# Order in which the second token group's operands take their buffers, in the SwiGLU stage of a two-layer encoder

## The reference, cut to what matters

```python
hid = jax.nn.silu(jnp.einsum('btd,df->btf', x, wg)) * jnp.einsum('btd,df->btf', x, wu)
return layer_norm(ALPHA * x + jnp.einsum('btf,fd->btd', hid, wd), ln2_g, ln2_b)
```

## Time and profile before

| | |
|---|---|
| median of 3 runs | 3147.59 us (3146.98 to 3153.67) |
| the profiled execution | 3151.21 us, its span 3149.4 us |
| PE busy (matmul) | 2922.8 us, 93% |
| DVE busy | 2149.4 us, 68% |
| POOL busy | 1725.8 us, 55% |
| ACT busy | 1249.3 us, 40% |
| mean granted TensorE clock | 0.961 |

### The profile page before, as it was taken

The page is one execution under the profiler, slowest core; times in us unless marked ns, Lnnn a source line. Parts: engine busy times, 40 slices in busy tenths (PEclk is TensorE's granted clock), DMA queues, the critical chain, the costliest instruction groups (busy, mean ns, idle before and its releaser), DMA issues. The chain is left out here.

```text
span 3149.4 us, 58397 instructions
## 1 busy us (share of the span) xinstructions
PE 2922.8 (93%) x20464; PEld 2660.4 (84%) x20464; DVE 2149.4 (68%) x3877; ACT 1249.3 (40%) x2422; POOL 1725.8 (55%) x1358
## 2 busy tenths in 40 slices
PE   7979998998999999999889699989989999999996
PEld 6956666887999999999879566668779999899996
DVE  6757776666666677777755577776486666877777
ACT  3324434435333344444333334444353333444442
POOL 2323332434766668788632233334266666788886
PEclk9989997999999999999989899989999999999998
DMA  4321114543222213323332211156432222222222
GB/s 170 126 82 42 51 39 152 158 128 129 88 80 84 88 62 101 100 98 101 116 122 94 78 48 41 33 166 179 132 116 81 80 80 80 74 101 97 101 89 88
DMA packets 175821, 304.91 MB, mean 97 GB/s; under 512 B 56080, under 2 KB 97296, under 8 KB 175344
## 3 DMA queue, kind: packets, MB, share of 16 engines
q1 hardware_dynamic: 165088, 271.70, 27.0%
q0 software_dynamic: 10576, 31.14, 2.5%
HBM read 248.34 MB, written 50.38 MB: 95 GB/s over the span
## 5 line engine op out<-in xcount | busy, mean ns | idle before, releaser
L2766 PE MATMUL PS<-xoh,woph 128*128 128x320 f32 (+1 forms) x2464 | 737.2, 299 | 20.9 <-issue 12.0
L2767 PE MATMUL PS<-xol,woph 128*128 128x320 f32 (+1 forms) x2464 | 735.0, 298 | 0.0
L2768 PE MATMUL PS<-xoh,wopl 128*128 128x320 f32 (+1 forms) x2464 | 733.9, 298 | 0.0
L1490 POOL TENSOR_TENSOR wopl<-T,woph 128x512 fp32r<-128x512 f32 x348 | 516.5, 1502 | 153.9 <-ACT woph L1955 153.9
L2766 PEld LDWEIGHTS PS<-xoh,woph 128*128 128x128 f32 x2464 | 467.7, 190 | 24.7 <-issue 18.0
L2767 PEld LDWEIGHTS PS<-xol,woph 128*128 128x128 f32 x2464 | 467.7, 190 | 0.1
L2768 PEld LDWEIGHTS PS<-xoh,wopl 128*128 128x128 f32 x2464 | 467.4, 190 | 0.0
L2766 PE MATMUL PS<-hidh,wdh 128*128 128x320 f32 (+1 forms) x1408 | 419.9, 298 | 11.4 <-DVE hidl L2616 7.8
L1437 POOL TENSOR_TENSOR Pl<-Pf,Ph 128x256 fp32r<-128x256 f32 (+5 forms) x174 | 219.0, 1265 | 384.5 <-DVE Ph L2349 384.5
L1955 ACT ACTIVATE woph<-T 128x512 fp32r<-128x512 f32 x348 | 217.3, 632 | 522.1 <-DVE T L2611 306.6
L2768 PE MATMUL PS<-hidh,wdl 128*128 128x320 f32 (+1 forms) x1408 | 419.1, 298 | 0.0
(11 more groups left out here) (476 smaller groups left out, 6642.7 us busy)
## 6 DMA issues: line engine op xcount, KB each, us to landing
ru<-in_W_FF SPq DMA_DIRECT2D x88, 512.0 KB, 4.0
rd<-in_W_FF SPq DMA_DIRECT2D x176, 256.0 KB, 2.6
rg<-in_W_FF SPq DMA_DIRECT2D x82, 512.0 KB, 4.1
sqt_scratch<-sqTs POOLq DMA_DIRECT2D x18, 512.0 KB, 4.2
hc<-out_H SPq DMA_DIRECT2D x18, 512.0 KB, 3.8
out_H<-yo POOLq DMA_DIRECT2D x18, 512.0 KB, 3.0
dkraw<-in_CKVT SPq DMA_DIRECT2D x16, 520.0 KB, 4.7
QS<-sqt_scratch SPq DMA_DIRECT2D x16, 512.0 KB, 3.5
```

The costliest lines, as they stand in the source:

```text
L1490: pool.tensor_tensor(wopl[k][:, :, :], w_whole(w, k, first), f(woph[k][:, :, :]), ALU.subtract)\
L2766: pe.matmul(out, wh, mh, start=start, stop=False)
L2767: pe.matmul(out, wh, ml, start=False, stop=False)
L2768: return pe.matmul(out, wl, mh, start=False, stop=stop)
```

## The change

The buffers of group 1 are taken in another order, and casts, sums and rests are placed to fit: A11 and A12 take the first two buffers (free with products 7 and 8), then S1, S2, S3, S4, and A22 takes the last. ACT casts A11 and A12 at steps 8 and 9 of turn 10, the sums at steps 10 to 13, and A22 at step 0 of turn 11. POOL takes the rests of A11 and A12 at steps 9 and 10 (before: 12 and 13), and that of A22 at step 0 of turn 11 (before: 1), one weight rest earlier. DVE builds the sums at steps 9 to 12, behind the step's weight sums (before: steps 7 to 10, ahead of them), takes the rests of S1, S2, S3 at steps 11, 12, 13 of turn 10 (before: S2 and S1 at 11 and 12, S3 at step 0 of turn 11), and that of S4 at step 2 of turn 11 as before. No instruction is added or dropped.

```diff
-X_SLOT = ((0, 1, 2, 3, 4, 5, 6), (4, 5, 1, 0, 2, 6, 3))
-X_BY_ACT = ((0, 1, 5, 3, 2, 6, 4), (3, 2, 4, 6, 0, 1, 5))
+X_SLOT = ((0, 1, 2, 3, 4, 5, 6), (0, 1, 3, 2, 4, 6, 5))
+X_BY_ACT = ((0, 1, 5, 3, 2, 6, 4), (0, 1, 3, 2, 4, 6, 5))
 X_BY_DVE = (("lo0", "lo1", "S1", "S2", "S4", "lo2", "lo3", "S3", "lo4", "lo5", "lo6", "g9", "x9"),
-            ("S1", "S2", "S3", "S4", "lo2", "lo3", "lo4", "lo6"))
+            ("S1", "S2", "S3", "lo3", "S4", "lo2", "lo4", "lo6"))
...
# POOL, turn
-                        if no == PAIRS - 1 and i in (12, 13):
-                            x_op_lo(i - 12)
-                        if no == PAIRS and i == 1:
+                        if no == PAIRS - 1 and i in (9, 10):
+                            x_op_lo(i - 9)
+                        if no == PAIRS and i == 0:
                             x_op_lo(5)
...
# ACT, turn
-                            x_op_hi(1, {8: 3, 9: 2, 10: 4, 11: 6, 12: 1, 13: 5}[i])
-                        if no == PAIRS - 1 and i == 11:
-                            x_op_hi(1, 0)
+                            x_op_hi(1, {8: 0, 9: 1, 10: 3, 11: 2, 12: 4, 13: 6}[i])
+                        if no == PAIRS and i == 0:
+                            x_op_hi(1, 5)
...
# DVE, turn
-                        if no == PAIRS and i in (0, 2):
-                            x_op_lo(1, 4 + i)
+                        if no == PAIRS and i == 2:
+                            x_op_lo(1, 6)
...
-                        if no == PAIRS - 1 and i in (7, 8, 9, 10):
-                            x_sum(1, (3, 2, 4, 6)[i - 7])
...
-                        if no == PAIRS - 1 and i in (11, 12):
-                            x_op_lo(1, i - 9)
+                        if no == PAIRS - 1 and i in (9, 10, 11, 12):
+                            x_sum(1, {9: 3, 10: 2, 11: 4, 12: 6}[i])
+                        if no == PAIRS - 1 and i >= 11:
+                            x_op_lo(1, {11: 3, 12: 2, 13: 4}[i])
```

## The result

The changed kernel took 3158.2 us (median of 20 runs, 3147.6 to 3167.3), the kernel before 3150.9 (20 runs, 3146.6 to 3159.3): a ratio of 1.0018 with a 95% interval of 1.0011 to 1.0026, that is 3.5 to 8.2 us slower. A second timing of both gave 1.0021 (1.0008 to 1.0035). The forecast was +5.9 us; the measured ratio is +5.7, the two medians are 7.3 apart, and so are the two profiled spans.

What follows compares the result with a forecast made beforehand. PE, busy 93% of the span, was taken as the bound, with DVE second and in arrears. PE's three waits go, DVE's arrears replace them: +2.95 us a layer, 3147.6 + 5.9 = 3153.5 us, range 3146 to 3159.

Steps and rivals of the forecast that it cites:

- The three waits of PE: Turn 11's products waiting for POOL's rests of A11, A12 and A22: waits of 3.04, 2.79 and 0.71 us would go.
- DVE's 2.2 us of new idle: Step 8 of turn 10: without the S1 and S2 sums DVE waits 1.36, 0.42 and 0.42 us for PE's products.
- The S1 sum of 3.4 us: Step 9 of turn 10: DVE's sum, 1.17 us of work, takes 3.4 because POOL's A11 rest holds SBUF first.
- rival B: Every moved instruction keeps its own row's duration, so POOL's rests cost DVE no more: 3149.4 to 3150.2 us; chance 0.13.
- PE's new waits: Down products 12, 14, 15, 0 and 2 wait for DVE: 1.1, 1.05, 4.3, 4.6 and 2.7 us, 13.8 a layer.
- the walk: Instruction-by-instruction reckoning of the hand-over, POOL and DVE taking turns at SBUF: down product 4 at 2760.80, old order 2757.85.
- The sum: Down product 4 compared between new and old order, both reckoned alike: +2.95 us a layer, +5.9 for two layers.
- the list of today's waits: PE's waits in the kernel before, from the trace: 8.5 us a layer, 10.4 with slow products and slower starts.
- The clock: Half-clock spells behind PE's new waits, costly over product 5: 0 to +1.6 us a layer, taken as 0.
- Rival C: The clock falls behind the new waits too, in both layers: 3155 to 3157 us; chance 0.18.
- Rival A: DVE keeps up at addition 13 and hid_lo, so the change is faster: 3130 to 3142 us; chance 0.14.
- Rival D: The order doesn't bite: another operand still comes last and PE's waits add up as before, 3147.6 us; chance 0.05.

Runs made afterwards that it cites:

- e2: Kernel before with its buffers, only DVE's sums and their rests placed as in the changed kernel; product 8 to down product 4 took 43.90 and 45.45 us.
- e3: Changed kernel with POOL's rests of A11, A12, A22 cut to 2 of 1056 columns; product 8 to down product 4 took 39.71 and 39.77 us.
- e4: Changed kernel with the rests of A11 and A12 on DVE, not POOL, at the same steps; product 8 to down product 4 took 41.55 and 41.56 us.
- e5: Changed kernel with S3's rest back at step 0 of turn 11, behind hid_lo; product 8 to down product 4 took 46.60 and 46.57 us.
- e1: Changed kernel with POOL's rests of A11 and A12 back at steps 12 and 13; product 8 to down product 4 took 43.55 us in both layers.
- e8: Kernel before with another buffer order, S3 summed in turn 11, quarters' rests on DVE, S4's on POOL; 3144.6 us against 3152.6, ratio 0.9981; again 0.9974.
- e6: Kernel before, same buffers, rests of A11, A12, A22 moved to DVE, S4's to POOL, S3's to step 1; 3148.0 us against 3152.6, ratio 0.9990.

## Why the prediction was right

**The three waits of PE** went, as said: product 0 starts right behind down product 15, nothing waits for POOL.

**DVE's 2.2 us of new idle:** 1.27 + 0.35 + 0.33 = 1.95 in the brackets. That this place costs what the change costs is shown by e2.

**The S1 sum of 3.4 us** took 3.54, the S3 sum 2.71 (2.64), S1's rest 2.33 (2.34), S3's rest 1.95 (1.94). Reading the meetings of POOL and DVE as turns was the step that mattered: by the rows taken at their face (rival B) D would have been 42.0 to 42.4; it was 43.97 or more in each of four readings. The Trainium skill's exclusive lock ("SBUF — State Buffer", section "SBUF: two separate sides") agrees with the trace, with e3 (1.25 for 3.54) and with e4, where two more instructions of 1.17 each on DVE made it earlier.

**PE's new waits,** each counted from when its first matmul could have started at the usual distance behind the last one (0.12 to 0.15 us, the "cadence" of the forecast): 1.15 at down product 12 (forecast 1.1), 0.87 at 14 (1.05), 4.0 at 15 (4.3), 2.8 at 0 (4.6), 2.4 at 2 (2.7). The one at down product 0 was 1.8 too large in the forecast, which had named over 4 us there as a sign, and the error cost nothing: products 0 to 2 ran partly at half clock, so PE came there 1.5 later. Hid_lo's release itself was right: down product 0 starts 33.5 us behind product 8, in the walk 33.9. In layer 0 the last wait is 0.9 only, as there the half clock lay over product 3 and down product 1 ahead of it; down product 2 itself starts 40.6 us behind product 8 in both layers, since addition 0 releases it.

**The sum,** +2.95 a layer, measured 2.82 where no spell follows. One term in the list of today's waits is off: the wait at down product 14 is 0.40 less its cadence by the earlier trace rows, not 0.51. The forecast, walk against walk, does not use it. That the time of 3158.2 lies inside the range of 3146 to 3159 owes something to its width: the forecast with its clock term ends at 3156.7, and the last 1.5 us are within the 3.3 by which the median of three runs lay low.

**The clock** is the term that was mis-sized. I took 0 in a range of 0 to 1.6 for each layer; it was 1.5 in one of the two layers in each profile of the changed kernel, and in e2, which has the same third wait, in one as well. The ground given was a misreading: the spells of the kernel before were said to begin within 1 us of the first long wait. In layer 0 this is so. In layer 1 the first wait (3.04) ended at 2739.60, product 0 ran at full clock, and the spell began at about 2744.7, behind the second wait (where 2742 to 2744 still has 1.00). Of the changed kernel's four hand-overs three had two spells: two of these had the second one behind down product 2, where nothing covers it, and one ahead of it, over product 3 and down product 1, where the wait for addition 0 does. The fourth had a single spell, twice as long, from 2749.7 to 2756.6 over down product 15 and products 0 to 2. So taking 0 was right in two hand-overs of four, and partly by luck; e5 had the uncovered spell in both of its layers, e2 in one of two, e1 and e4 in none, and e3 has one ahead of down product 2 in both. With it the sum is 2 x 2.85 + 1.5 = 7.2, which is the difference in D; the ratios (5.7 and 6.6) can't tell 5.9 from 7.2. Rival C is thus half true. The Trainium skill, page "TensorE: Matmul & The Clock Gate" (section "What's actually happening"), says that the default state is throttled and activity releases it. The trace agrees as far as each of these spells begins in a long wait or behind one; which wait brings one, these runs don't settle.

**Rival A** fell: DVE was 3 us late at product 11's work and never caught up before hid_lo. **Rival D** fell with it.

## What to carry to other kernels

A wait of the bound engine is worth only what is left when the engine in second place has had its say: before a wait is removed, look whether the next engine has any idle bracket in that stretch, and what it will be late with. Where POOL and DVE both read SBUF, book their instructions on one calendar. Then a move to the engine that looks overloaded can help (e4, e8). A repair that brings one engine sooner to its work can harm where it then waits for a third engine, and wins nothing where the moved work still stands ahead of what the bound engine waits for next (e5).
A kernel with single times 15 us apart can still be read to 0.1 us, if the stretch between two fixed instructions is compared in place of the whole, and if the granted clock inside it is looked at: an uncovered spell changed D by 1.4 to 1.5 us.

## What was not expected of the hardware

- The stretch D repeated to 0.02 us in two profiled executions each of the kernel before and of e8, while their whole times differed by 4.8 and 4.5 us; in the kernel before it is even the same in both layers within 0.04, although its half-clock spells lie in different places (PE's wait for A12 was 1.5 us shorter in layer 0 and the matmuls around it that much slower).
- A second half-clock spell came behind the third of three waits in two hand-overs of the changed kernel, ahead of it in one, and not at all in one: D 43.97 or 45.50, nothing in between in four readings.
- POOL started 0.15 us before DVE where the walk had DVE first, and D came out 2.2 us longer than in the walk (e6); that the one caused the other is not shown.
